# The fold of the output weights in three fp32r products instead of f32, its rows split ahead of it, the pooled rows loaded before the transforms, and frequency row 64 stored over GpSimd's queue

## The chip, the cores and the metric

One core of one Trainium2 chip runs the whole program. The metric is the device time of one execution in microseconds; a kernel's number is the median of its runs.

## The reference

The block works on two sequences, 2048 and 1024 tokens of width 1024, with the same weights:

```
h = rmsnorm(x, g1);  z = h @ w_in
za = z[:, :512] in 4 heads of 128:   f = real(fft2(za over tokens and channels));  ya = f @ w_fourier[h]
zb = z[:, 512:] in 4 groups of 128:  yb = ((mean over a window) - zb) @ w_pool[g] * pool_scale
x = x + concat(ya, yb) @ w_out
h = rmsnorm(x, g2);  x = x + (silu(h @ w_gate) * (h @ w_up)) @ w_down
y = rmsnorm(x, gf)
```

## The kernel before

All 3072 tokens pass through five stages in one program, and each engine has one instruction stream through all of them: input projection (`project_in`), Fourier mixing (`mix`), output projection (`project_out`), and the FFN (`ffn`). Nearly all products are made in three fp32r parts: a factor is rounded to fp32r by ScalarE (`hi`), VectorE subtracts that from the raw value (`lo`), and `three_products` adds hi·hi, hi·lo and lo·hi on TensorE, one instruction each.

The change lies in `mix`. It runs over eight units n = 0 to 7: four of the long sequence, four of the short one. A unit is a block of 128 rows (half the frequencies, cosine or sine part, of two heads) over all tokens of its sequence. VectorE folds its tokens (`fold`), TensorE transposes the folds (`turn_folds`), ScalarE and VectorE split them (`round_uv`, `rest_of_uv` write `uv_hi`, `uv_lo`), and TensorE multiplies them by tables at levels 0, 1, the base and, for the long sequence, 2 (`level_products`, `transform`). ScalarE copies the results to the unit's slot (`zy`, `zy_late`), and SyncE stores the slot to `y_scr` in HBM (`store_unit`). The slots of units 4 to 7 are loaded on SyncE's queue once the pooled values (`win`, stored over GpSimd's queue) have landed.

Between the parts of the units TensorE makes side products, in the order of `SIDE`, placed by `EARLY_SIDE` and `LATE_SIDE`, both indexed by unit:

- `F00` to `F31` and `G00` to `G31` fold the Fourier weights and the pooling weights into the rows of `w_out`: 16 products of 128x128 by 128x512, Fij for head i and column half j, Gij for pooling group i. Their left factors are `spread_w` and `wp_t`, their right ones the rows `wm` (mixed) and `wb` (pooled) of `w_out`. They are made in f32, two TensorE instructions each, on line 1324. ScalarE copies the F products (line 1196), VectorE the G products (line 1241). They go to two banks in turn, so a product waits for the copy of the one two before it (F01 for that of F00). The copies of F go to memory that the slots of units 0 and 1 hold, so they wait for these units' stores (`y_stored[0]`).
- `lone0` and `lone1` are the Fourier transform of frequency row 64 of the channels, which is stored apart from the units: TensorE, then GpSimd's four small multiplications, TensorE, TensorE; `store_lone` puts it into `y_scr` with four small DMAs on SyncE's queue, just before the stores of unit 3 and of unit 7.

The folded rows are split as well (`round_w` on ScalarE, `rest_of_w` on VectorE, lines 1202 and 1234; in `project_out` lines 1599 and 1809), and so is the first tile of y (`y_hi`, `y_lo`, lines 1218 and 1246), which is loaded from `y_scr` (line 1142) once units 0 to 3 and row 64 of the long sequence are stored. `project_out` begins on TensorE when `y_lo` and the first of the eight row blocks of weights are split, and takes them one by one. Each engine does its part in the order written in `scalar`, `vector`, `tensor`, `sync` and `gpsimd`.

Of the kernel before, what the change touches and what calls it, by code (L numbers as in the profile page):

```python
# [23 lines left out]
F32 = mybir.dt.float32  # L24
# [4 lines left out]
P = 128  # L29
# [827 lines left out]
class Mixer:  # L857
# [7 lines left out]
    FIRST_OF_TWO = 7  # L865
    EARLY_SIDE = ((), (1,), (3,), (4,), (6, 7), (11, 12), (16, 17), (20, 21))
# [3 lines left out]
    def __init__(self, nc, ahead, ctx, w_out, w_fourier, channel, z_scr, pool_gain, g2):  # L870
# [41 lines left out]
        self.wm = sb("wm", [P, HEADS, D], F32, ahead.w_place + 32 * K)  # L912
        self.chan = sb("chan", [P, channel_places().join1.stop - P], F32, ahead.folds_at)
# [10 lines left out]
        self.wm_loaded = sem("wm_loaded")  # L924
        self.wb_loaded = sem("wb_loaded")
# [60 lines left out]
    def load_mixed_rows(self, sp):  # L986
        sp.dma_start(self.wm[:, :, :], self.sources[0][0:HEADS * P, :].rearrange("(h p) n -> p h n", p=P)).then_inc(self.wm_loaded, DMA)

    def load_pooled_rows(self, sp):
        sp.dma_start(self.wb[:, :, :], self.sources[0][HEADS * P:, :].rearrange("(g p) n -> p g n", p=P)).then_inc(self.wb_loaded, DMA)  # L990
# [64 lines left out]
def mix(nc, ctx, ahead, mixer, z_scr, y_scr, w_pool):  # L1055
# [16 lines left out]
    spread_w = sb("spread_w", [P, HEADS, P], F32, 59 * K + 512)  # L1072
    MS = [S // P for S in SEQS]
# [11 lines left out]
    wm_loaded, wb_loaded = mixer.wm_loaded, mixer.wb_loaded  # L1085
    pool_w_loaded = sem("pool_w_loaded")
    lone_chain = sem("lone_chain")
    lone_turned = sem("lone_turned")
# [10 lines left out]
    def sync(sp):  # L1099
        def store_lone(q):  # L1100
            S, m = SEQS[q], MS[q]
            mixer.wait_side(sp, SIDE.index(f"lone{q} c"))
            for h in range(HEADS):
                sp.dma_start(y_scr[h, HALF_P, tok0[q]:tok0[q] + S].rearrange("(a b) -> a b", a=m),  # L1104
                             lone_out[q][h * m:(h + 1) * m, :]).then_inc(lone_stored[q], DMA)

        def store_unit(n):
            q, u = divmod(n, UNITS)
            S, k = SEQS[q], u % 2
            sp.wait_ge(out_done, mixer.stage(n, 3 - q))  # L1110
            for side in range(2):
                sp.dma_start(y_scr[u // 2 * 2 + side, k * (HALF_P + 1):(k + 1) * HALF_P, tok0[q]:tok0[q] + S],  # L1112
                             mixer.slot(n)[side * HALF_P + k:(side + 1) * HALF_P, :]).then_inc(y_stored[n // 2], DMA)

        sp.wait_ge(ahead.z_ready, TOKENS // HALF * KT)
        sp.dma_start(wp[:, :, :], w_pool.rearrange("g c d -> c g d")).then_inc(pool_w_loaded, DMA)
        for s in range(HEADS):
            sp.wait_ge(ahead.z_stored[s], TOKENS // HALF * DMA)
        for i in range(2):
            sp.wait_ge(ahead.d_stored[i], 2 * (TOKENS // HALF) * DMA)  # L1120
        sp.wait_ge(ahead.group_done, 4 * (TOKENS // HALF))
        mixer.load_unit(sp, z_scr, 1, 0)
        mixer.load_unit(sp, z_scr, 1, 1)
        for n in range(N):
            if n == UNITS - 1:
                store_lone(0)
            if n == N - 1:
                store_lone(1)
            store_unit(n)
            if n == 0:  # L1130
                mixer.load_unit(sp, z_scr, 1, 2)
                mixer.load_unit(sp, z_scr, 1, 3)
                mixer.load_lone(sp, 1)
            if n == 1:
                mixer.load_pooled_rows(sp)
            if n == UNITS - 1:
                for pair in range(2):
                    sp.wait_ge(y_stored[pair], 4 * DMA)
                sp.wait_ge(lone_stored[0], HEADS * DMA)
                for t in range(4):  # L1140
                    src = y_scr[:, :, t * P:(t + 1) * P].rearrange("c p s -> p c s")
                    sp.dma_start(y_raw[t // 2][:, :, t % 2 * P:(t % 2 + 1) * P], src).then_inc(ahead.y_loaded, DMA)

    def gpsimd(pool):
        done = 0
        for q in range(2):
# [6 lines left out]
            done += 2  # L1153
            pool.wait_ge(lone_chain, done)
            pool.tensor_tensor(g[:, 0:m], a[:, 0:m], a[:, m:], ALU.subtract).then_inc(lone_turned, 1)
            pool.tensor_tensor(g[:, m:], b[:, 0:m], b[:, m:], ALU.add).then_inc(lone_turned, 1)
            pool.wait_ge(lone_turned, 2 * q + 2)

    def scalar(act):
# [43 lines left out]

        for n in range(N):
# [11 lines left out]
            if n == N - 1:  # L1216
                act.wait_ge(ahead.y_loaded, 4 * DMA)
# [10 lines left out]
        round_w(1)  # L1228
        round_w(2)

    def vector(dve):
# [16 lines left out]

        for n in range(N):
# [6 lines left out]
            if n == N - 1:  # L1256
                rest_of_w(0)
                rest_of_y()
# [7 lines left out]
        rest_of_w(1)  # L1266

    def tensor(pe):
# [15 lines left out]
        def side(a):  # L1284
# [18 lines left out]
            elif name[0] == "l":  # L1303
# [6 lines left out]
                elif name[-1] == "b":  # L1310
                    pe.wait_ge(lone_turned, 2 * q + 2)
# [5 lines left out]
            else:  # L1317
                i, c = int(name[1]), int(name[2])
                if name == "F00":
                    pe.wait_ge(wm_loaded, DMA)  # L1320
                if name == "G00":
                    pe.wait_ge(wb_loaded, DMA)
                left, right = (spread_w, wm) if name[0] == "F" else (wp_t, wb)
                mm = pe.matmul(ps[:, :], left[:, i, :], right[:, i, c * HALF:(c + 1) * HALF], start=True, stop=True)
# [1734 lines left out]
```

## Time and profile before

| | us |
|---|---|
| median of 3 runs | 2498.29 (2497.23 to 2500.4) |
| the profiled execution | 2496.63 |
| its span | 2494.8 |
| TensorE busy | 2477.2 |
| VectorE busy | 1670.7 |
| ScalarE busy | 957.8 |
| GpSimd busy | 162.3 |

The span is the part of the execution that the profile covers; 1.8 us lie around it. The granted clock of TensorE was 0.999 of full speed over the span. All times below are from the span's start; the units' transforms lie from 291 us to 342 us. A matmul's duration covers its way through the array, so neighbours overlap: the cost of one is the step from its start to the next one's. ScalarE's and VectorE's instructions overlap a little too.

### The profile page before, as it was taken

Reading aid. Unit: us, or ns where it says so; the run is one execution under the profiler, and the core shown is the slowest. Engines: PE = TensorE matmul, PEld = TensorE weight load, DVE = VectorE, ACT = ScalarE, POOL = GpSimd, SP = SyncE. Lnnn points to the kernel's source line nnn. Section 1 sums busy time; section 2 is a strip of 40 time slices with the busy share of each in tenths; the row PEclk is TensorE's granted clock in tenths of the full one; section 3 lists DMA queues with packets and bytes.
Section 4 is the critical chain, followed back from the end, with each engine's and each line's share of the span. In section 5 each row is a group of like instructions: output and inputs, shape, how many; then the busy total and the mean of one; then the engine's idle time right before and its main releaser. Section 6 shows DMA issues by size and latency. Waiting matters only on the chain.

```text
span 2494.8 us, 32121 instructions
## 1 busy us (share of the span) xinstructions
PE 2477.2 (99%) x11133; PEld 2047.8 (82%) x11133; DVE 1670.7 (67%) x2595; ACT 957.8 (38%) x1825; POOL 162.3 (7%) x214
## 2 busy tenths in 40 slices
PE   9999999999999999999999999999999999999998
PEld 7888878887888888888888888888888888888887
DVE  5555678778767677777677686776764564455565
ACT  5533466667333333433333343333332232233333
POOL 2655400000000000000000000000000000000000
PEclk9999999999999999999999999999999999999999
DMA  6433667667323233432232442222346654354554
GB/s 184 115 84 99 212 218 248 239 239 277 136 100 109 97 109 110 182 126 109 80 117 99 155 157 96 110 109 80 126 177 220 239 207 168 114 199 147 191 193 148
DMA packets 154309, 381.99 MB, mean 153 GB/s; under 512 B 11928, under 2 KB 48120, under 8 KB 145012
## 3 DMA queue, kind: packets, MB, share of 16 engines
q1 hardware_dynamic: 145808, 350.86, 40.6%
q0 software_dynamic: 7984, 29.89, 3.2%
q8 instruction: 51, 0.84, 0.1%
q14 instruction: 34, 0.28, 0.0%
q10 hardware_dynamic: 432, 0.14, 0.0%
HBM read 254.22 MB, written 126.62 MB: 153 GB/s over the span
## 4 chain that ended last, share of the span: by engine, by line
PE 95%; DVE 2%; DMA 1%; issue 1%; ACT 1%; SPq 1%; DVEq 0%
PE bank L351 31%; PE bank L352 31%; PE bank L353 31%; PE bank L1968 1%; DMA a_raw<-ha_scr 0%; DMA y_scr<-zy_late 0%; DVE a_lo L2540 0%; DMA y_raw<-y_scr 0%; PE bank L765 0%; DMA xin<-in_x 0%; SPq L1112 0%; SPq L1104 0%; DVE x L1769 0%; ACT a_hi L2349 0%; PE bank L1039 0%
## 5 line engine op out<-in xcount | busy, mean ns | idle before, releaser
L351 PE MATMUL bank<-a_hi,w_hi 128*128 128x512 f32 x1848 | 719.5, 389 | 2.4 <-DVE w_lo L2551 1.6
L353 PE MATMUL bank<-a_hi,w_lo 128*128 128x512 f32 x1848 | 719.0, 389 | 0.0
L352 PE MATMUL bank<-a_lo,w_hi 128*128 128x512 f32 x1848 | 718.9, 389 | 0.0
L351 PEld LDWEIGHTS bank<-a_hi,w_hi 128*128 128x128 f32 x1848 | 346.9, 188 | 76.4 <-DVE w_lo L2551 2.8
L353 PEld LDWEIGHTS bank<-a_hi,w_lo 128*128 128x128 f32 x1848 | 346.9, 188 | 72.3
L352 PEld LDWEIGHTS bank<-a_lo,w_hi 128*128 128x128 f32 x1848 | 346.9, 188 | 71.6
L351 PE MATMUL bank<-t_hi,s_hi 128*128 128x512 f32 x924 | 359.4, 389 | 0.0
L352 PE MATMUL bank<-t_lo,s_hi 128*128 128x512 f32 x924 | 359.4, 389 | 0.0
L353 PE MATMUL bank<-t_hi,s_lo 128*128 128x512 f32 x924 | 359.4, 389 | 0.0
L2362 ACT ACTIVATE w_hi<-t_raw 128x512 fp32r<-128x512 f32 x256 | 162.0, 633 | 463.0 <-PE bank L353 379.5
L2701 DVE TENSOR_TENSOR s_lo<-s_raw,s_hi 128x512 fp32r<-128x512 f32 x231 | 156.2, 687 | 232.7 <-ACT s_hi L2437 232.6
L2437 ACT ACTIVATE s_hi<-s_raw 128x512 fp32r<-128x512 f32 x231 | 133.4, 620 | 320.6 <-DMA s_raw<-s_scr 320.6
L353 PEld LDWEIGHTS bank<-t_hi,s_lo 128*128 128x128 f32 x924 | 173.5, 188 | 36.0
L352 PEld LDWEIGHTS bank<-t_lo,s_hi 128*128 128x128 f32 x924 | 173.5, 188 | 36.0
L351 PEld LDWEIGHTS bank<-t_hi,s_hi 128*128 128x128 f32 x924 | 173.5, 188 | 36.0
L2551 DVE TENSOR_TENSOR w_lo<-t_raw,w_hi 128x512 fp32r<-128x512 f32 x256 | 176.0, 688 | 30.0 <-ACT w_hi L2362 26.3
L2551 DVE TENSOR_TENSOR w_lo<-w_raw,w_hi 128x512 fp32r<-128x512 f32 x192 | 132.1, 688 | 87.6 <-ACT w_hi L2362 87.5
L2362 ACT ACTIVATE w_hi<-w_raw 128x512 fp32r<-128x512 f32 x192 | 120.2, 626 | 121.3 <-PE bank L353 121.0
L351 PE MATMUL bank<-h_hi,win_hi 128*128 128x512 f32 x380 | 149.5, 394 | 0.0
L353 PE MATMUL bank<-h_hi,win_lo 128*128 128x512 f32 x380 | 148.0, 389 | 0.0
L352 PE MATMUL bank<-h_lo,win_hi 128*128 128x512 f32 x380 | 147.9, 389 | 0.0
L2322 POOL DMA_DIRECT2D acc<-x_scr x6 | 4.5, 754 | 1655.2 <-PE bank L353 1655.2
(266 smaller groups left out, 3143.3 us busy)
## 6 DMA issues: line engine op xcount, KB each, us to landing
s_scr<-sums_out SPq DMA_DIRECT2D x33, 1792.0 KB, 5.9
s_raw<-s_scr SPq DMA_DIRECT2D x42, 1024.0 KB, 5.1
w_raw<-in_w_gate SPq DMA_DIRECT2D x64, 512.0 KB, 3.6
w_raw<-in_w_up SPq DMA_DIRECT2D x64, 512.0 KB, 4.4
wd_staged<-in_w_down SPq DMA_DIRECT2D x121, 256.0 KB
a_raw<-ha_scr SPq DMA_DIRECT2D x21, 1024.0 KB, 4.9
s_raw<-s_scr SPq DMA_DIRECT2D x21, 768.0 KB, 4.7
x<-in_x SPq DMA_DIRECT2D x24, 512.0 KB, 4.5
```

Of the source, the lines that this page charges most:

```text
L351: pe.matmul(out, w_hi, m_hi, start=first, stop=False, **checks)
L352: pe.matmul(out, w_hi, m_lo, start=False, stop=False, **checks)
L353: return pe.matmul(out, w_lo, m_hi, start=False, stop=last, **checks)
L1968: mm = pe.transpose(t_ps[(slot % 2) * 2 + k][:, i, :], xn[:, slot % 2, d * P:(d + 1) * P], eye[:, :])
L2322: pool.dma_start(acc[b][half][:, :, :], src).then_inc(acc_loaded[b][half], DMA)
L2362: act.activation(w_hi[j][:, :], src, ACT.Copy).then_inc(w_hi_done, 1)
L2437: act.activation(s_hi[c][:, k - 4 * c, :], s_raw[c][:, k - 4 * c, :], ACT.Copy).then_inc(s_hi_done, 1)
L2551: dve.tensor_tensor(w_lo[j][:, :], src, w_hi[j][:, :].bitcast(F32), ALU.subtract).then_inc(w_ready, 1)
L2701: dve.tensor_tensor(s_lo[c][:, k - 4 * c, :], s_raw[c][:, k - 4 * c, :], s_hi[c][:, k - 4 * c, :].bitcast(F32), ALU.subtract).then_inc(s_r ...
```

## The change

- The left factors and the rows are split before use: ten pieces (`ROWS_SPLIT`), `spread` and `wp` of 512 columns, four blocks of mixed and four of pooled rows, 1024 columns each. ScalarE rounds (`round_rows`), VectorE subtracts (`rest_of_rows`), both at the end of the unit that `SPLIT_AT` names. `lo` parts are written over the raw values.
- Each of the 16 side products is made by `three_products`, three instructions.
- The pooled rows (`wb`, 2 MB) are issued on SyncE's queue behind `wp`, before the queue waits for the pooled values and loads units 4 to 7; before they were issued after the store of unit 1. Mixed and pooled rows share a semaphore, and the second load waits for the first.
- The four small stores of row 64 of each sequence are issued by GpSimd, after its multiplications, when the last copy of `lone` is made.
- `round_w(1)` moves ahead of the rounding of y in unit 7, `rest_of_w(0)` from unit 7 to the end of unit 6, `rest_of_w(1)` from behind unit 7's copies to ahead of the split of y.

```diff
+    ROWS_SPLIT = ("spread", "mixed0", "mixed1", "mixed2", "wp", "mixed3", "pooled0", "pooled1", "pooled2", "pooled3")
+    SPLIT_AT = ((0, 1), (2,), (3, 4), (5,), (6,), (7, 8), (9,), ())
...
     def load_pooled_rows(self, sp):
+        sp.wait_ge(self.rows_loaded, DMA)
...
         sp.dma_start(wp[:, :, :], w_pool.rearrange("g c d -> c g d")).then_inc(pool_w_loaded, DMA)
+        mixer.load_pooled_rows(sp)
         for s in range(HEADS):
             sp.wait_ge(ahead.z_stored[s], TOKENS // HALF * DMA)
...
-            if n == UNITS - 1:
-                store_lone(0)
-            if n == N - 1:
-                store_lone(1)
             store_unit(n)
...
-            if n == 1:
-                mixer.load_pooled_rows(sp)
...
     def gpsimd(pool):
+                pool.dma_start(y_scr[h, HALF_P, tok0[q]:tok0[q] + S].rearrange("(a b) -> a b", a=m),
+                               lone_out[q][h * m:(h + 1) * m, :]).then_inc(lone_stored[q], DMA)
...
             if n == N - 1:
+                round_w(1)
                 act.wait_ge(ahead.y_loaded, 4 * DMA)
...
+            for r in mixer.SPLIT_AT[n]:
+                round_rows(r)
-        round_w(1)
         round_w(2)
...
+        def rest_of_rows(r):
+            raw, hi, lo = rows_split(r)
+            dve.wait_ge(rows_hi_done, r + 1)
+            dve.tensor_tensor(lo, raw, hi.bitcast(F32), ALU.subtract).then_inc(rows_ready, 1)
...
             if n == N - 1:
-                rest_of_w(0)
+                rest_of_w(1)
                 rest_of_y()
...
-        rest_of_w(1)
+            for r in mixer.SPLIT_AT[n]:
+                rest_of_rows(r)
+            if n == N - 2:
+                rest_of_w(0)
...
-                mm = pe.matmul(ps[:, :], left[:, i, :], right[:, i, c * HALF:(c + 1) * HALF], start=True, stop=True)
+                rows = mixer.ROWS_SPLIT.index(("mixed" if name[0] == "F" else "pooled") + name[1])
+                pe.wait_ge(rows_ready, rows + 1)
+                    mm = three_products(pe, ps[:, :], spread_hi[:, i, :], spread_lo[:, i, :], mixer.wm_hi[:, i, of],
+                                        mixer.wm_lo[:, i, of], True, True)
```

VectorE, from the splits of unit 6's second group to the first weights of `project_out`, before (`uv_lo` is the split of folds, `wout_raw_94` a copy of a G product, `wout_lo` a split of folded rows):

```order
L1051 TENSOR_TENSOR uv_lo_120<-bank,uv_hi_118 128x384 [waits uv_hi_done]
L1241 TENSOR_SCALAR wout_raw_94<-bank 128x512 [waits side_made] x2
L1051 TENSOR_TENSOR uv_lo_121<-bank,uv_hi_119 128x256 [waits uv_hi_done]
L1241 TENSOR_SCALAR wout_raw_94<-bank 128x512 [waits side_made]
L1051 TENSOR_TENSOR uv_lo_121<-bank,uv_hi_119 128x384 [waits uv_hi_done]
L1241 TENSOR_SCALAR wout_raw_94<-bank 128x512 [waits side_made] x3
L1234 TENSOR_TENSOR wout_lo_107<-wout_raw_93,wout_hi 128x2x512 [waits wout_hi_done]
L1246 TENSOR_TENSOR y_lo_113<-y_raw_51,y_hi_109 128x1024 [waits y_hi_done]
L1241 TENSOR_SCALAR wout_raw_94<-bank 128x512 [waits side_made] x2
L1234 TENSOR_TENSOR wout_lo_107<-wout_raw_93,wout_hi 128x2x512 [waits wout_hi_done]
```

and now (line 1283 is the split of the rows, 1272 the copy, 1265 and 1277 the splits of folded rows and of y):

```order
L1057 TENSOR_TENSOR uv_lo_120<-bank,uv_hi_118 128x384 [waits uv_hi_done]
L1272 TENSOR_SCALAR wout_raw_94<-bank 128x512 [waits side_made] x2
L1283 TENSOR_TENSOR wb_lo<-wb,wb_hi 128x1024 [waits rows_hi_done] x2
L1057 TENSOR_TENSOR uv_lo_121<-bank,uv_hi_119 128x256 [waits uv_hi_done]
L1272 TENSOR_SCALAR wout_raw_94<-bank 128x512 [waits side_made]
L1057 TENSOR_TENSOR uv_lo_121<-bank,uv_hi_119 128x384 [waits uv_hi_done]
L1272 TENSOR_SCALAR wout_raw_94<-bank 128x512 [waits side_made] x2
L1283 TENSOR_TENSOR wb_lo<-wb,wb_hi 128x1024 [waits rows_hi_done]
L1265 TENSOR_TENSOR wout_lo_107<-wout_raw_93,wout_hi 128x2x512 [waits wout_hi_done]
L1272 TENSOR_SCALAR wout_raw_94<-bank 128x512 [waits side_made]
L1265 TENSOR_TENSOR wout_lo_107<-wout_raw_93,wout_hi 128x2x512 [waits wout_hi_done]
L1277 TENSOR_TENSOR y_lo_113<-y_raw_51,y_hi_109 128x1024 [waits y_hi_done]
```

Three splits of pooled rows stand between the G copies, and both first splits of folded rows stand ahead of the split of y.

SyncE's queue, from `wp` to the load of y, before (`zy_95` is the slot of units 4 to 7, `lone_out` row 64):

```order
L1116 DMA wp<-in_w_pool 128x4x128 [waits z_ready]
L967 DMA zy_95<-z_scr 64x1024 [waits d_stored0,z_stored3,d_stored1,z_stored2,group_done,z_stored1,z_stored0]
L1112 DMA y_scr<-zy 64x2048 [waits out_done]
L967 DMA zy_95<-z_scr 64x1024 x4
L1112 DMA y_scr<-zy 63x2048 [waits out_done]
L990 DMA wb<-in_w_out 128x4x1024
L1112 DMA y_scr<-zy_late 64x2048 [waits out_done]
L1104 DMA y_scr<-lone_out_129 16x128 [waits side_done]
L1104 DMA y_scr<-lone_out_129 16x128 x3
L1112 DMA y_scr<-zy_late 63x2048 [waits out_done]
L1142 DMA y_raw_51<-y_scr 128x8x128 [waits lone_stored0,y_stored1,y_stored0]
```

and now:

```order
L1132 DMA wp<-in_w_pool 128x4x128 [waits z_ready]
L996 DMA wb<-in_w_out 128x4x1024 [waits rows_loaded]
L972 DMA zy_95<-z_scr 64x1024 [waits d_stored0,z_stored3,d_stored1,z_stored2,group_done,z_stored1,z_stored0]
L1128 DMA y_scr<-zy 64x2048 [waits out_done]
L972 DMA zy_95<-z_scr 64x1024 x4
L1128 DMA y_scr<-zy 63x2048 [waits out_done]
L1128 DMA y_scr<-zy_late 64x2048 [waits out_done]
L1128 DMA y_scr<-zy_late 63x2048 [waits out_done]
L1153 DMA y_raw_51<-y_scr 128x8x128 [waits lone_stored0,y_stored1,y_stored0]
```

The load of the pooled rows has gone from between the stores of units 1 and 2 to ahead of the loads of units 4 to 7, and the stores of row 64 have left the queue. (A second DMA of the same kind behind a row, without a wait of its own, is left out here.)

## Rows read from the trace of the kernel before

**Rows 1.** The page's busy time by engine: us (share of the span) x instructions

```profile
PE 2477.2 (99%) x11133; PEld 2047.8 (82%) x11133; DVE 1670.7 (67%) x2595; ACT 957.8 (38%) x1825; POOL 162.3 (7%) x214
```

**Rows 2.** Waits from 190 to 360 us: engine, line, releaser, total us, times, longest

```profile
PE bank L1324 <- ACT wout_raw L1196: 2.0, 1, 2.0
...
PE bank L351 <- DVE wout_lo L1234: 0.7, 1, 0.7
PE bank L351 <- DVE y_lo L1246: 0.6, 1, 0.6
...
PE bank L1324 <- DVE wout_raw L1241: 0.2, 1, 0.2
```

**Rows 3.** ScalarE in order of time, in brackets its idle time and who ended it

```profile
312.63 0.64 ACT L1172 ACTIVATE zy_late<-bank 128x512 f32<-128x512 f32 x1 [1.30 <-PE bank L353]
...
318.59 0.60 ACT L1196 ACTIVATE wout_raw<-bank 128x512 f32<-128x512 f32 x1 [2.10 <-DMA y_scr<-zy]
...
333.66 1.04 ACT L1202 ACTIVATE wout_hi<-wout_raw 128x1024 fp32r<-128x1024 f32 x1
...
339.93 1.06 ACT L1218 ACTIVATE y_hi<-y_raw 128x1024 fp32r<-128x1024 f32 x1 [1.84 <-DMA y_raw<-y_scr]
```

**Rows 4.** The issue of DMAs on SyncE's queue in order of time

```profile
299.88 2.37 SPq L967 DMA_DIRECT2D zy<-z_scr  x4
...
309.71 0.79 SPq L1112 DMA_DIRECT2D y_scr<-zy  x2
310.54 0.77 SPq L990 DMA_DIRECT2D wb<-in_w_out  x1
...
315.97 4.24 SPq L1104 DMA_DIRECT2D y_scr<-lone_out  x4
...
331.20 3.66 SPq L1142 DMA_DIRECT2D y_raw<-y_scr  x4
```

**Rows 5.** Line 1324 over the span: count, duration ns min/median/max, first and last start

```profile
L1324 PE MATMUL bank<-wm,spread_w x16: 592/592/697, 315.3 to 329.1; 128*128 128x512 f32 x16
```

**Rows 6.** TensorE in order of time: start, us, engine, line, operation, tiles, count

```profile
309.62 0.47 PE L351 MATMUL bank<-tab_hi,uv_hi 128*128 128x512 f32 x1
309.93 0.39 PE L352 MATMUL bank<-tab_lo,uv_hi 128*128 128x512 f32 x1
...
311.97 0.39 PE L352 MATMUL bank<-tab_lo,uv_hi 128*128 128x512 f32 x1
...
322.43 2.83 PE L1324 MATMUL bank<-wm,spread_w 128*128 128x512 f32 x6
...
325.23 0.28 PE L352 MATMUL bank<-tab_lo,uv_hi 128*128 128x256 f32 x1
325.34 0.28 PE L353 MATMUL bank<-tab_hi,uv_lo 128*128 128x256 f32 x1
...
336.50 0.28 PE L352 MATMUL bank<-tab_lo,uv_hi 128*128 128x256 f32 x1
...
342.30 0.50 PE L351 MATMUL bank<-wout_hi,y_hi 128*128 128x512 f32 x1 [0.57 <-DVE y_lo L1246]
```

**Rows 7.** DMA issues, 283 to 284 us

```profile
y_scr<-win POOLq DMA_DIRECT2D x1, 260.0 KB, 5.6
```

**Rows 8.** DMA issues, 296 to 297 us

```profile
y_scr<-win POOLq DMA_DIRECT2D x1, 260.0 KB, 2.9
```

**Rows 9.** VectorE in order of time

```profile
305.48 0.68 DVE L1013 TENSOR_TENSOR scratch<-zy 128x512 f32<-128x512 f32 x1
...
308.61 0.69 DVE L1051 TENSOR_TENSOR uv_lo<-bank,uv_hi 128x512 fp32r<-128x512 f32 x1 [0.26 <-ACT uv_hi L1045]
...
344.49 5.76 DVE L1809 TENSOR_TENSOR wout_lo<-wout_raw,wout_hi 128x1024 fp32r<-128x1024 f32 x5
```

**Rows 10.** 2 us stretches: PE, PEld, DVE, ACT, POOL busy, TensorE's clock, DMA share, GB/s

```profile
294.00:296.00 2.00, 2.00 (x20) 2.00 (x18) 0.51 (x1) 2.00 (x5) 1.84 (x3) 1.00 0.18 55
```

**Rows 11.** DMA issues, 310.5 to 311 us: count, KB, us to landing

```profile
wb<-in_w_out SPq DMA_DIRECT2D x1, 2048.0 KB, 13.4
```

More of the change, by code:

```diff
@@ L1072, in mix @@
     spread_w = sb("spread_w", [P, HEADS, P], F32, 59 * K + 512)
+    wp_lo = sb("wp_lo", [P, 4, P], F32R, 61 * K + 512)
+    wp_hi = sb("wp_hi", [P, 4, P], F32R, 29 * K + 512)
+    spread_lo = sb("spread_lo", [P, HEADS, P], F32R, 59 * K + 512)
+    spread_hi = sb("spread_hi", [P, HEADS, P], F32R, 52 * K + 512)
     MS = [S // P for S in SEQS]
@@ L1099, in sync @@
     def sync(sp):
[L1100 to L1105, printed above, removed]
         def store_unit(n):
@@ L1144, in gpsimd, with store_lone @@
     def gpsimd(pool):
-        done = 0
+        def store_lone(q):
+            S, m = SEQS[q], MS[q]
+            mixer.wait_side(pool, SIDE.index(f"lone{q} c"))
+            for h in range(HEADS):
+                pool.dma_start(y_scr[h, HALF_P, tok0[q]:tok0[q] + S].rearrange("(a b) -> a b", a=m),
+                               lone_out[q][h * m:(h + 1) * m, :]).then_inc(lone_stored[q], DMA)
         for q in range(2):
@@ L1152, in gpsimd @@
             pool.tensor_tensor(b, cs, turn[:, m:3 * m], ALU.mult).then_inc(lone_chain, 1)
[L1153 to L1157, printed above, removed]
+            pool.wait_ge(lone_chain, 4 * q + 2)
+            pool.tensor_tensor(g[:, 0:m], a[:, 0:m], a[:, m:], ALU.subtract).then_inc(lone_chain, 1)
+            pool.tensor_tensor(g[:, m:], b[:, 0:m], b[:, m:], ALU.add).then_inc(lone_chain, 1)
+            pool.wait_ge(lone_chain, 4 * q + 4)
+            store_lone(q)
     def scalar(act):
@@ L1202, in round_w, with round_rows @@
             act.activation(w_hi[:, :, d, :], w_raw[0][:, :, d, :], ACT.Copy).then_inc(ahead.w_hi_done, 1)
+        def round_rows(r):
+            name = mixer.ROWS_SPLIT[r]
+            raw, hi, _ = rows_split(r)
+            if name == "mixed0":
+                act.wait_ge(rows_loaded, DMA)
+            elif name == "pooled0":
+                act.wait_ge(rows_loaded, 2 * DMA)
+            elif name in ("spread", "wp"):
+                mixer.wait_side(act, SIDE.index(name))
+            act.activation(hi, raw, ACT.Copy).then_inc(rows_hi_done, 1)
         for n in range(N):
@@ L1318, in side @@
                 i, c = int(name[1]), int(name[2])
[L1319 to L1323, printed above, removed]
-                mm = pe.matmul(ps[:, :], left[:, i, :], right[:, i, c * HALF:(c + 1) * HALF], start=True, stop=True)
+                rows = mixer.ROWS_SPLIT.index(("mixed" if name[0] == "F" else "pooled") + name[1])
+                pe.wait_ge(rows_ready, rows + 1)
+                of = slice(c * HALF, (c + 1) * HALF)
+                if name[0] == "F":
+                    mm = three_products(pe, ps[:, :], spread_hi[:, i, :], spread_lo[:, i, :], mixer.wm_hi[:, i, of],
+                                        mixer.wm_lo[:, i, of], True, True)
+                else:
+                    mm = three_products(pe, ps[:, :], wp_hi[:, i, :], wp_lo[:, i, :], mixer.wb_hi[:, i, of],
+                                        mixer.wb_lo[:, i, of], True, True)
             mm.then_inc(side_made, 1)
```

28 lines of the change are left out of this document (21 added, 7 removed).

## The prediction

> **What bounds the kernel now.** The page's busy times come first: TensorE is at work in 2477.2 of 2494.8 us [rows 1]. So the kernel can gain in two ways: less work on TensorE, or fewer stalls of it. The waits of the stretch from 190 to 360 us show the stalls: 2.0 us on ScalarE's copies of folded rows, 0.7 on the split of folded rows, 0.6 on the split of y and 0.2 on a copy of VectorE [rows 2], 3.5 us in all. Everything the change touches lies there. After that the timelines of the engines say what stands behind each stall.
>
> The largest is F01's. It waits for the copy of F00, and ScalarE began that only at 318.59, after 2.10 us of waiting for the store of unit 1 to land [rows 3]. That store was issued at 309.71, with the 2 MB of pooled rows right behind it [rows 4]. The wait on y has the same origin: y's load began at 331.20 [rows 4] and ScalarE took it at 339.93, again after waiting for a DMA [rows 3].
>
> **The products.** There are 16 of them; the mixed half stands in the trace as 16 matmuls of 592 ns, two for each product [rows 5], the pooled half likewise. Their cost is the step, not the duration. Six such instructions (three products) begin at 322.43, the second instruction of the next group begins at 325.23, and a 256-column step is 0.11 to 0.12 us [rows 6]. So three products take 2.80 - 0.12 = 2.68 us, one takes 0.89. In fp32r a 512-column step is (311.97 - 309.93) / 9 = 0.227 us [rows 6], three are 0.68. That saves 0.21 us a product, 16 x 0.21 = 3.4 us on TensorE's own path. The wait for the split rows adds to that only where a split is late, which is counted below.
>
> **The stalls that go.** Without the pooled rows, the store of unit 1 and that of unit 2 share the queues with nothing new. From 309.71 to 331.20 the queue moved three stores of about 1 MB and the 2 MB of rows: 5 MB in 21.5 us. Three fifths of that is 12.9 us, so units 1 to 3 are stored by about 323 instead of 331. Unit 1's store, landed at 318.6 before, should land near 315.5; F00's product ends at about 316.3, so F01's 2.0 us go. If none of this came true and unit 1 landed at 318.5 again, 1.9 us of stall would stay: that is the other end of this term. The 4.24 us in which the queue issued row 64's four stores [rows 4] go as well. y's load then begins at 323 and lands, with the 8.7 us of before (331.20 to 339.93), at about 332. ScalarE asks for it at 336. It is hidden with 4 us to spare, and even a load that lands at 338 costs only 0.1. The waits on y, on the first folded rows and on the copy (0.6 + 0.7 + 0.2) go in their old form. Gone: 3.5 us.
>
> GpSimd issues row 64's stores from about 314.3, in some 2.3 us of its own. Pooled values over this queue landed 2.9 to 5.6 us after issue [rows 7, 8], so row 64 is there by 322.5, just ahead of unit 3's store; 5 us more would still be hidden. The store of row 64 of the short sequence is as free: before, it stood in front of the store of unit 7.
>
> **The pooled rows in their new place.** Now 2 MB are in flight from 292.5, when the last pooled values are still to be stored, and the queue may load units 4 and 5 only when these have landed: issued at 296.8, landed 2.9 us later [rows 8]; the queue went on at 299.88 [rows 4]. The DMA engines have room, 18% busy from 294 to 296 [rows 10], so I let the rows be in by 299.5 and keep unit 4's arrival at about 305: cost 0. At a busy time the same kind of store took 5.6 us [rows 7]; the cost of that is rival 1.
>
> The Trainium skill speaks against this move. Its page "DMA: Bandwidth & Descriptors", section "SWDGE vs HWDGE vs iDMA", has each DMA engine take its hardware-fed and software-fed queues in turn, so the small store would share with the rows in front of it rather than pass or queue behind them. By that rule it is about 1 us late while the rows last, unit 4 comes at 306, and the sum below would be -2.0 instead of -3.0.
>
> **The stalls that come.** The ten splits cost ScalarE 0.95 to 1.04 us for each of the eight blocks of 1024 columns [rows 3] and VectorE 5.76 / 5 = 1.15 us [rows 9]. They are put at the ends of units, where ScalarE waits for TensorE anyway: 1.30 us before 312.63 [rows 3] cover most of unit 2's 1.5. VectorE is tighter, and I followed the three engines from unit to unit with these durations (the same reckoning, done for the kernel before, ends within 0.3 us of the trace).
>
> - Unit 1's split lies between the fold of unit 4 and the split of unit 3's folds at 308.61, before which VectorE idled 0.26 us [rows 9]. It comes 0.9 us later; TensorE, which took it at 309.62 [rows 6], had 0.3 us in hand. With 0.1 won before that: 0.4 us of stall.
> - G10 needs pooled block 1, whose subtraction stands behind the copy of G01. After G01, TensorE has 1.07 us of other work; VectorE needs 0.2 to see the product, 0.6 for the copy (a 512-column instruction is 0.69 long [rows 9]) and 1.15: 0.9 us of stall.
> - From the end of G20 to the first product of `project_out` TensorE has little work and VectorE much. Before, 336.38 (the row at 336.50 less one step) to 342.30 [rows 6] held 5.9 us, of which 0.8 idle; less 3 x 0.21 for three products, 4.5 us of work remain. VectorE must in this time split unit 7's folds, copy G11 and G20 (0.6 each), split block 3 (1.15), split w0 (1.15), copy G21 (0.6), split w1 (1.15) and then y (1.2): with the small waits for ScalarE, 6.7 us. So 2.2 us of stall, most of it on `y_lo`. Behind it nothing more is late: w2 is split before its turn at 2.7 us after the start, so the 0.7 of before has no heir.
> - Small ones at F21, G01 and around the copies: 0.4 us.
>
> Sum of the new ones: 0.4 + 0.9 + 2.2 + 0.4 = 3.9 us.
>
> **The sum.** -3.4 (products) - 3.5 (old stalls) + 3.9 (new stalls) = -3.0 us. The profiled execution of 2496.6 would become 2493.6. It lies 1.7 us under the median of the runs shown, so for the median I take 2498.3 - 3.0 = 2495.3. Later stages are TensorE's without a gap of this kind, so the 3.0 us should stay.
>
> **The rivals.** All of them turn on the new place of the pooled rows or on VectorE.
>
> 1. The pooled rows hold up the pooled values. With 5.6 us for that last store [rows 7] unit 4 comes 2.7 us late. VectorE began its fold at 305.48 [rows 9] and would begin at 307; that delays unit 3's split and TensorE by 2.0 us. Result -1.0: 2497.3.
>
> 2. The other side: the pooled rows take the 13.4 us that they took before [rows 11] and are in flight to 306. Loads of units 4 and 5 share with them and unit 4 lands at 309. Each us past 305 costs one us on TensorE, since fold, split and level 0 of unit 3 stand in one line; break-even is at 308. At 309 the result is +1.0, and with the stores behind them late too (unit 1 at 321) +1.5: 2499.8.
>
> 3. More is won than I reckon, since the new stalls on VectorE are my own reckoning and no row shows them. If only half of the 3.9 us came, the result would be -5.0: 2493.3. Against it: the order on VectorE leaves no room between G20 and y.
>
> 4. The change doesn't do what it says: the three-part product takes as long as the f32 one, 0.89. Then nothing is saved, but the stalls shrink too, since TensorE comes later to each of them: -0.9, 2497.4. Against it stand 9 steps in a row of 0.227 with new weights for each [rows 6].
>
> **How the numbers follow.** Forecast 0.50, rival 1 0.19, rival 2 0.13, rival 3 0.15, rival 4 0.03. What a measurement of this kernel can tell from no change is about 0.2%, 5.0 us; the runs before lie 3.2 us apart. Only rival 3 at its far end reaches that downwards: 0.11. Upwards only rival 2 with everything late: 0.04. Same: 0.85. The range goes down to rival 3 and a little below, for the scatter, 2492.3, and up to rival 2, 2499.9.
>
> **What would show it.** In the changed kernel's trace: line 1324's f32 products gone, three steps of 0.227 in their place; no wait of ScalarE for a DMA before the copy of F00, nor before `y_hi`; a stall near 0.9 us before G10 and one of 1 to 2 us on `y_lo` before `project_out`; the first product of `project_out` at about 340.1 (before 342.30), without the gap of 0.7 us after it. I am wrong if VectorE waits for unit 4's load, if GpSimd's stores of row 64 hold up y, or if the stall on `y_lo` is missing or above 3 us.

## The result, and the profile after

The changed kernel takes 2501.68 us (median of 22 runs, 2498.45 to 2505.49), the kernel before in the same batch 2497.76 (22 runs, 2496.31 to 2501.4): ratio 1.0015, 95% interval 1.0009 to 1.0021. It is slower by about 3.9 us; 2495.3 was forecast, with 2499.9 as the upper end. The profiled execution took 2500.15 us, its span 2498.4, 3.6 more than before.

TensorE's busy time has hardly changed against [rows 1], by the page:

```profile
PE 2476.6 (99%) x11149; PEld 2051.5 (82%) x11149; DVE 1682.0 (67%) x2605; ACT 965.7 (39%) x1835; POOL 165.4 (7%) x222
```

So the time has gone into stalls. TensorE's waits from 290 to 350 us (line, releaser, total us, times, longest) answer to [rows 2]:

```profile
PE bank L1045 <- DVE uv_lo L1057: 2.9, 1, 2.9
PE bank L351 <- ACT wout_raw L1213: 1.6, 1, 1.6
PE bank L351 <- DVE y_lo L1277: 1.3, 1, 1.3
PE bank L351 <- DVE wb_lo L1283: 1.1, 1, 1.1
PE bank L351 <- DVE wout_raw L1272: 0.3, 2, 0.2
PE bank L1354 <- DVE wout_raw L1272: 0.3, 1, 0.3
PE bank L351 <- DVE uv_lo L1057: 0.2, 1, 0.2
```

They come to 7.7 us, against 3.5. The largest is one that the forecast had at 0.4. F01's wait (the second row) should have gone and is still 1.6. F01 waits for the copy of F00, the product right before it: up to F10 the side products share one bank, and only from then on do they wait for the copy of the one two before.

What stands behind the first is seen on SyncE's queue, in order of time, beside [rows 4]:

```profile
292.51 0.57 SPq L996 DMA_DIRECT2D wb<-in_w_out  x1
302.97 2.38 SPq L972 DMA_DIRECT2D zy<-z_scr  x4
...
312.91 0.79 SPq L1128 DMA_DIRECT2D y_scr<-zy  x2
...
330.94 3.65 SPq L1153 DMA_DIRECT2D y_raw<-y_scr  x4
```

The loads of units 4 and 5 are issued 3.1 us later than before (299.88), and the store of unit 1 3.2 us later. y's load begins where it did. The DMA issues from 285 to 330 us (KB each, us from issue to landing) say why; they answer to [rows 8, 11]:

```profile
wb<-in_w_out SPq DMA_DIRECT2D x1, 2048.0 KB, 10.7
...
y_scr<-win POOLq DMA_DIRECT2D x1, 260.0 KB, 6.3
...
y_scr<-lone_out POOLq DMA_DIRECT2D x4, 8.0 KB, 3.8
```

The pooled rows need 10.7 us, to 303.2. The last store of the pooled values, issued at 296.48, falls into their time and takes 6.3 us instead of 2.9, and SyncE may not load unit 4 before it has landed. It landed at 302.8, about when the rows did. So VectorE, which had no wait there in [rows 9], waits for unit 4:

```profile
307.73 0.69 DVE L1019 TENSOR_TENSOR scratch<-zy 128x512 f32<-128x512 f32 x1 [2.07 <-DMA zy<-z_scr]
```

TensorE in order of time, beside [rows 6]:

```profile
312.49 0.41 PE L1045 MATMUL bank<-eye,zy_late 128*128 128x128 f32 x2 [2.95 <-DVE uv_lo L1057]
312.65 0.48 PE L351 MATMUL bank<-tab_hi,uv_hi 128*128 128x512 f32 x1
...
313.43 0.47 PE L351 MATMUL bank<-tab_hi,uv_hi 128*128 128x512 f32 x1
313.70 0.63 PE L352 MATMUL bank<-tab_lo,uv_hi 128*128 128x512 f32 x1
...
316.69 0.56 PE L353 MATMUL bank<-tab_hi,uv_lo 128*128 128x512 f32 x1
317.08 0.38 PE L1045 MATMUL bank<-eye,zy 128*128 128x128 f32 x2
...
347.13 0.50 PE L351 MATMUL bank<-wout_hi,y_hi 128*128 128x512 f32 x1 [1.30 <-DVE y_lo L1277]
```

After the stall of 2.95 us the steps grow from 0.23 to 0.43 us. The nine matmuls from 313.43 to 317.08 take 3.65 us, where nine steps of 0.227 would take 2.04: 1.6 us more. The windows of this kernel (busy us by engine, granted clock, DMA share, GB/s) name the reason in the column PEclk: the clock granted in 314 to 316 us is 0.50, so 1.2 GHz instead of 2.4.

```profile
312.00:314.00 2.00, 1.51 (x7) 1.33 (x8) 1.46 (x4) 1.07 (x2) 0.00 (x0) 0.91 1.03 248
314.00:316.00 2.00, 2.00 (x6) 1.54 (x6) 1.90 (x5) 0.78 (x2) 0.00 (x0) 0.50 1.11 239
316.00:318.00 2.00, 2.00 (x10) 1.31 (x9) 2.00 (x4) 0.72 (x2) 0.00 (x0) 0.74 0.93 286
322.00:328.00 6.00, 4.62 (x25) 3.75 (x26) 4.60 (x10) 5.39 (x13) 0.00 (x0) 1.00 0.56 199
```

Hold on to the last row: while TensorE and the queue wait for stores, the DMA engines are at 0.56.

Which of these delays sets the time? The stall and the slow steps make TensorE 4.5 us late, but behind them it still waits 1.56 us at F01, for a copy that waits for unit 1's store. ScalarE's copy of F00 and TensorE's F01, first before (F00's copy is in [rows 3]), then in the changed kernel:

```profile
319.24 1.98 PE L1324 MATMUL bank<-wm,spread_w 128*128 128x512 f32 x4 [2.01 <-ACT wout_raw L1196]
```

```profile
322.61 0.60 ACT L1213 ACTIVATE wout_raw<-bank 128x512 f32<-128x512 f32 x1 [1.45 <-DMA y_scr<-zy]
323.26 0.50 PE L351 MATMUL bank<-wm_hi,spread_hi 128*128 128x512 f32 x1 [1.56 <-ACT wout_raw L1213]
```

The copy and F01 are both 4.02 us later than before. So there are two late paths from the same cause. One goes over unit 4, VectorE and the stall; alone it would have brought F01 at 321.7. The other goes over SyncE's queue, whose store of unit 1 was issued 3.2 us late and took 9.7 us instead of 8.9; it brought F01 at 323.26. The second is the longer by 1.56 us, so it sets the time from F01 on.

### The profile page after: what moved, and what is told of

The parts are those of the page before. It is cut to its first block, busy times and chain, and to the rows that moved or that the text cites. A ratio compares the mean times of both kernels' runs of the same rounds, so it can differ in the third digit from the quotient of the medians.

```text
span 2498.4 us, 32187 instructions
## 1 busy us (share of the span) xinstructions
PE 2476.6 (99%) x11149; PEld 2051.5 (82%) x11149; DVE 1682.0 (67%) x2605; ACT 965.7 (39%) x1835; POOL 165.4 (7%) x222
## 4 chain that ended last, share of the span: by engine, by line
PE 93%; DMA 2%; DVE 2%; ACT 1%; POOL 1%; issue 1%; SPq 0%; POOLq 0%; ACTq 0%; DVEq 0%
PE bank L351 30%; PE bank L353 30%; PE bank L352 30%; DMA y_scr<-win 1%; PE bank L2010 1%; DVE a_lo L2582 0%; DMA tab_raw<-in_table 0%; POOL win L322 0%; DMA y_scr<-zy 0%; ACT a_hi L2391 0%; SPq L972 0%; PE bank L765 0%; DMA xin<-in_x 0%; DMA a_raw<-ha_scr 0%; POOL win L332 0%
```

## The experiments

Each is against the kernel before, run in the same batch on the same chip; experiments 1 to 4, 5 to 8, 9 to 11 and 12 are four batches, so that runs of different batches are compared by their ratios. "After" is the changed kernel.

**1. Rows at the old place.** After, with the pooled rows loaded behind unit 1's store again:

```diff
-        mixer.load_pooled_rows(sp)
...
+            if n == 1:
+                mixer.load_pooled_rows(sp)
```

> The changed kernel with the pooled rows issued after the store of unit 1, as before; all else of the change stays. Theory 1 (the rows, in flight from 292.5 us, hold up the last pooled values, so the queue, unit 4's load, its fold and TensorE are late, and the long idle time halves TensorE's clock): no VectorE wait for unit 4's load, the 2.95 us stall and the stretch at clock 0.5 gone, median 1 us under the kernel before, about 5 us under the changed one. Theory 2 (the new splits on VectorE cause the long stall, since unit 1's split stands between the fold and unit 3's split): the stall stays near 3 us and the time within 1 us of the changed kernel's. Theory 3 (GpSimd's stores of row 64 hold up the rest): the same, time as the changed kernel's.

Measured 2498.95 us, ratio 1.0003 (0.9994 to 1.0012). The rows' early place costs 2.7 us of the 3.9; the two intervals overlap a little, and experiment 2 has the same cause clear of noise. Theory 1 is right about the stall and the clock, but not in size: 1 us under the kernel before was expected, and it is 1.3 above, within noise. TensorE's wait for `uv_lo` is 0.7 and its clock 1.00 throughout.

**2. Rows early, nothing else.** Before, with only this move:

```diff
+        sp.wait_ge(mixer.wm_loaded, DMA)
+        mixer.load_pooled_rows(sp)
...
-            if n == 1:
-                mixer.load_pooled_rows(sp)
```

> The kernel before with one thing changed: the pooled rows issued behind wp. Theory 1: the last store of pooled values lands about 6 us after issue instead of 2.9, the queue goes on at 303, VectorE waits 2 us for unit 4, TensorE about 2 us; if that idle time also halves the clock, 1.7 us more: 2 to 4 us over the kernel before. Theory 2: no loss, since no split is added; the time of before or 1 us less, as the rows are out of the way of the units' stores.

Measured 2502.86, ratio 1.0018 (1.0009 to 1.0027): the move alone costs about 5 us, where Theory 1 had 2 to 4. The path over unit 4 is shorter than expected: the last store of pooled values takes 5.1 us, VectorE waits 1.1, TensorE 0.8 with its clock at 1.00. The price is paid on the other path. This is ScalarE's wait before it copies F00:

```profile
ACT wout_raw L1196 <- DMA y_scr<-zy: 5.4, 1, 5.4
```

Unit 1's store was issued at 311.65 and landed at 322.5, although nothing but other stores stood behind it. TensorE waited 5.3 us for F00's copy.

**3. The products alone.** Experiment 1, with row 64 stored over SyncE's queue as before; no part of the change but the products and their splits is left:

```diff
-            store_lone(q)
...
+            if n == UNITS - 1:
+                store_lone(0)
+            if n == N - 1:
+                store_lone(1)
```

> The three-part products and their splits alone: pooled rows in their old place and row 64 on SyncE's queue. Theory 1: close to the run with the rows in their old place, 0 to 1 us under the kernel before: products -3.4 us, new stalls on VectorE about +3.9, of the old stalls the one on F01 stays near 1.7. Theory 3: clearly faster than the run that has row 64 on GpSimd's queue, by 1 us or more.

Measured 2497.75, ratio 0.9998 (0.9989 to 1.0007): zero. Against experiment 1 (2498.95) GpSimd's queue for row 64 isn't shown to gain or to cost anything. TensorE's largest waits here:

```profile
PE bank L351 <- ACT wout_raw L1217: 2.2, 1, 2.2
PE bank L351 <- DVE y_lo L1281: 1.3, 1, 1.3
PE bank L351 <- DVE wb_lo L1287: 1.1, 1, 1.1
PE bank L1045 <- DVE uv_lo L1057: 0.7, 1, 0.7
```

All its waits sum to 6.0 us, 2.5 more than before, and the span is 0.3 longer. So the products save about 2.2 in this execution.

**4. TensorE kept busy.** After, with 13 idle matmuls where TensorE waits for unit 3's split:

```diff
+                if n == 2 and g == 2:
+                    pe.wait_ge(out_done, mixer.stage(1, 0))
+                    for _ in range(13):
+                        pe.matmul(bank[1][:, :], tab_hi[:, 0:P], tab_hi[:, 0:HALF], start=True, stop=True)
```

> The changed kernel with 13 additional matmuls of 128x128 by 128x512 that nothing uses, 13 x 0.227 = 2.95 us, on TensorE where it waits for unit 3's split. Theory 1 with the clock as a part of the loss: the clock stays at 1.00 from 313 to 317 us, level 0 of unit 3 steps 0.227 us all through instead of 0.43, time about 1.7 us under the changed kernel. If the slow steps have another cause (transfers, reads of the tables), they stay at 0.43 and the time is that of the changed kernel.

Measured 2502.39, ratio 1.0017 (1.0008 to 1.0026). The clock is 1.00 from 308 to 320 us and no step is 0.43, but nothing is won. The test is a weak one: in this execution VectorE waited only 1.3 us for unit 4 (2.07 in after), so the stall that the idle matmuls filled would have been shorter. And what they can win ends at F01, which waits for unit 1's store whatever TensorE did before:

```profile
PE bank L351 <- ACT wout_raw L1213: 2.8, 1, 2.8
```

The wait is 2.78 us here and 1.56 in after. The half clock is real in after's profiled execution, but by the trace it cost nothing there: without its 1.6 us TensorE would have waited 1.6 us longer at F01.

**5. No pooled rows at all.** Before, without their load; the pooled products take columns of the table instead:

```diff
-            if n == 1:
-                mixer.load_pooled_rows(sp)
...
-                if name == "G00":
-                    pe.wait_ge(wb_loaded, DMA)
-                left, right = (spread_w, wm) if name[0] == "F" else (wp_t, wb)
-                mm = pe.matmul(ps[:, :], left[:, i, :], right[:, i, c * HALF:(c + 1) * HALF], start=True, stop=True)
+                left, right = (spread_w, wm) if name[0] == "F" else (wp_t, None)
+                idle = mixer.places[mixer.plan_of(N - 1)["levels"][0], "sin"]
+                rows = right[:, i, c * HALF:(c + 1) * HALF] if right is wm else tab_hi[:, idle:idle + HALF].bitcast(F32)
+                mm = pe.matmul(ps[:, :], left[:, i, :], rows, start=True, stop=True)
```

> The kernel before without the load of the pooled rows (2 MB); the products of the pooled groups take 512 columns of the table as their right factor instead, of the same size and kind, so the last four row tiles of the output weight are wrong and nothing else changes in work. Theory A, that of the prediction: the rows behind unit 1's store slow it and all that follows, so without them it lands near 315.5 us, F01's wait (2.0 us before) goes and the load of y starts at 323 instead of 331: 2494.5 us, 3.3 us less. Theory B, from the runs so far: what is issued behind a store doesn't slow it, and the stores of units 1 and 3 are slow by themselves (63 rows each, DMA share near 0.58 for 8 us): unit 1's store lands at 318 and later as before, F01's wait stays within 0.5 us, the load of y starts at 328 or later; within 1 us of before.

Measured 2499.84, ratio 1.0006 (0.9997 to 1.0015). Theory A falls: ScalarE waits for unit 1's store longer than before, and y's load begins at 328.47 instead of 331.20, not at 323.

```profile
ACT wout_raw L1194 <- DMA y_scr<-zy: 3.9, 1, 3.9
```

Theory B is right that the rows aren't what slows the store, and wrong in size: issued at 309.52, it landed at 320.4, 1.8 us later than with the rows behind it. Where unit 2's store follows directly (here, in experiments 2 and 4 and in after) it took 9.7 to 10.9 us from issue, with the rows between (before, experiments 1 and 3) 8.9 to 9.6. Why is open. The kernel's median is not shown to differ from before's.

**6. Stores of 48 and 15 rows.** Before, with each 63-row store of the odd units cut in two, and the waits on the stores raised from 4 to 6 to match:

```diff
-                sp.dma_start(y_scr[u // 2 * 2 + side, k * (HALF_P + 1):(k + 1) * HALF_P, tok0[q]:tok0[q] + S],
-                             mixer.slot(n)[side * HALF_P + k:(side + 1) * HALF_P, :]).then_inc(y_stored[n // 2], DMA)
+                for a, b in (((1, 49), (49, HALF_P)) if k else ((0, HALF_P),)):
+                    sp.dma_start(y_scr[u // 2 * 2 + side, k * HALF_P + a:k * HALF_P + b, tok0[q]:tok0[q] + S],
+                                 mixer.slot(n)[side * HALF_P + a:side * HALF_P + b, :]).then_inc(y_stored[n // 2], DMA)
```

> The kernel before with each 63-row store of the odd units issued as 48 and 15 rows. 
Measured 2494.81, ratio 0.9989 (0.9980 to 0.9998): 2.6 us faster, with an interval from 0.5 to 5.0. The window from 322 to 326 us, first of before, then of this kernel, shows DMA share and GB/s at the end:

```profile
322.00:326.00 4.00, 4.00 (x20) 2.39 (x19) 2.61 (x6) 3.04 (x7) 0.00 (x0) 1.00 0.59 239
```

```profile
322.00:326.00 4.00, 4.00 (x22) 2.81 (x22) 3.04 (x7) 3.12 (x9) 0.00 (x0) 1.00 1.03 408
```

The share rises from 0.59 to 1.03 and the rate from 239 to 408 GB/s: this is what one expects if the stores of 63 rows used nine of sixteen engines (9/16 is 0.56). ScalarE takes F00 at 316.67 instead of 318.59, TensorE's wait for it is 0.4, and y's load starts at 328.84. The waits of 0.6 and 0.7 us around `y_lo` were expected to go; 0.3 and 0.7 are left. The Trainium skill has the rule, in "DMA: Bandwidth & Descriptors", section "Why a DMA increments its semaphore by 16 and not by 1": a hardware-fed DMA takes the largest number of engines, up to 16, that divides the slowest dimension of both its sides. For 63 that is 9, for 48 it is 16, for 15 it is 15. With its shares of 0.59 and 1.03 the trace agrees, but it doesn't show 48 and 15 apart, and no run cuts the 63 rows otherwise: that the row counts help, and not just that there are two transfers for one, rests on this rule and on the 0.59.

**7. Rows behind unit 5.** After, with the pooled rows issued after the loads of units 4 and 5:

```diff
         mixer.load_unit(sp, z_scr, 1, 1)
+        mixer.load_pooled_rows(sp)
```

> The kernel after with the pooled rows issued behind the loads of units 4 and 5 (near 300 us) instead of ahead of them. If they cost by holding up the last store of the pooled values and with it unit 4 (6.3 us against 2.9 to landing, unit 4 at 308 against 305.5): the store lands in 3 us again, VectorE doesn't wait for unit 4, TensorE's 2.95 us wait for uv_lo and its half clock go, 3 us off: 2498.5 us. Rival: 2 MB more ahead of unit 0's and unit 1's stores hold these up, F01's wait of 1.6 us grows to 4 or more: no gain, 2501 us or more.

Measured 2503.82, ratio 1.0026 (1.0017 to 1.0035). The rival was right. The pooled values' store lands in 2.3 us and VectorE doesn't wait for unit 4, but 2 MB now stand ahead of the stores of units 0 and 1, and unit 1's lands 16.1 us after its issue:

```profile
PE bank L351 <- ACT wout_raw L1213: 6.0, 1, 6.0
```

With one path mended and the other made longer, the kernel is slower: the store's path is the one that counts here. The rows ahead of a store delayed it in each of these runs; these two moves only chose who pays.

**8. Products and 48 and 15 rows.** Experiment 3 with the edit of 6, its core being

```diff
+                for a, b in (((1, 49), (49, HALF_P)) if k else ((0, HALF_P),)):
```

> Three-part products alone (pooled rows at their old place, row 64 over SyncE's queue: 0.0 us against before) with the stores of 48 and 15 rows. If the 63-row stores hold up y and F01: the waits for wout_raw (2.2 us) and y_lo (1.3 us) go while the products' 3.4 us stay, wb_lo's 1.1 us remains: 2493.5 us, 4 less than before. If they don't: 2497.7 as without the split.

Measured 2496.42, ratio 0.9996 (0.9987 to 1.0005), where 2493.5 was expected. It is 1.6 us more than the stores alone, with overlapping intervals. F01's wait is gone, those for `y_lo` (1.3) and `wb_lo` (1.1) are unchanged: `y_lo` is late by VectorE's own order here, not by the load of y.

**9. Splits at other places.** Experiment 8 with

```diff
-    SPLIT_AT = ((0, 1), (2,), (3, 4), (5,), (6,), (7, 8), (9,), ())
+    SPLIT_AT = ((0, 1, 2), (3,), (4, 5), (), (6, 7), (8, 9), (), ())
```

> As the run with three-part products and stores of 48 and 15 rows, but with the ten splits behind other units: pieces 0 to 2 behind unit 0, 3 behind unit 1, 4 and 5 behind unit 2, 6 and 7 behind unit 4, 8 and 9 behind unit 5. There TensorE still waited 1.3 us for y_lo, 1.1 for wb_lo of the second pooled block, 0.7 for uv_lo and 0.7 in small pieces. If the place of the splits is what costs: the 1.1 for wb_lo goes, about 1 us off: 2495.4 us against 2496.4. If it is the work itself on VectorE and ScalarE, which has no free place: the waits turn up elsewhere (uv_lo of units 3 and 5, y_lo) with the same sum, 2496.4 us.

Measured 2494.88, ratio 0.9987 (0.9978 to 0.9996). The interval overlaps that of 8, so a gain from the places isn't shown. The waits moved: `wb_lo` is gone, `y_lo` 0.6, while 0.9 for a copy of VectorE and 0.7 for copies of ScalarE came.

**10. Only the mixed rows in three parts.** Experiment 8 with the pooled products in f32 again, and the splits of the mixed rows at the places of experiment 9:

```diff
-    SPLIT_AT = ((0, 1), (2,), (3, 4), (5,), (6,), (7, 8), (9,), ())
+    SPLIT_AT = ((0, 1, 2), (3,), (4,), (), (), (), (), ())
...
-                    mm = three_products(pe, ps[:, :], wp_hi[:, i, :], wp_lo[:, i, :], mixer.wb_hi[:, i, of],
-                                        mixer.wb_lo[:, i, of], True, True)
+                    pe.wait_ge(rows_loaded, 2 * DMA)
+                    mm = pe.matmul(ps[:, :], wp_t[:, i, :], wb[:, i, of], start=True, stop=True)
```

> Stores of 48 and 15 rows, and three-part products for the mixed rows (F) alone: the eight pooled products (G) stay f32 and the splits of wp and of the pooled rows go (4.9 us of VectorE less). If the splits' work is what ate the gain: 1.6 us for the F products stay (8 x 0.2), the waits for wb_lo (1.1) and most of that for y_lo (1.3 to 0.3) go: 2493.5 us, 1.3 less than the stores alone (2494.8). Rival: the two halves are alike and the F half's splits cost what they save too (uv_lo 0.7 and small ones): 2494.8, as the stores alone.

Measured 2493.50, ratio 0.9984 (0.9975 to 0.9993). It has the lowest median of all, some 4 us under before, and hits the 2493.5 expected, though `y_lo` keeps 0.8 where 0.3 was expected. Its interval overlaps those of 8 and 9 and that of 6, with which it shared no batch, so that leaving out the pooled half gains isn't shown. Its waits from 290 to 350 us sum to 2.0:

```profile
PE bank L1045 <- DVE uv_lo L1057: 1.0, 1, 1.0
PE bank L351 <- DVE y_lo L1282: 0.8, 1, 0.8
PE bank L1370 <- DVE wout_raw L1277: 0.2, 1, 0.2
```

**11. After with 48 and 15 rows.** The same edit in the changed kernel, with the waits on the stores raised to match:

```diff
-                    sp.wait_ge(y_stored[pair], 4 * DMA)
+                    sp.wait_ge(y_stored[pair], 6 * DMA)
```

> The kernel after with the 63-row stores issued as 48 and 15 rows. If the early place of the pooled rows costs by delaying unit 4 and the stores alike: F01's wait (1.6 us) goes, while the wait for uv_lo of unit 3 (2.9 us) and the half clock behind it stay: 2499.5 us, 2 less than after and 2 more than before. Rival: with the stores quick the early rows cost nothing more: 2496.4 us, as the same kernel with the rows at their old place.

Measured 2498.91, ratio 1.0004 (0.9995 to 1.0013). As expected, F01's wait goes, and the 3.2 us for `uv_lo` stay, with a granted clock of 0.51 in 312 to 314 us. With the store's path shortened, the path over unit 4 is the one that counts.

**12. Half the rows early.** Experiment 11, with pooled row tiles 0 and 1 early and 2 and 3 behind unit 1's store (the second argument picks the half; the wait for the second load is left out here):

```diff
-        mixer.load_pooled_rows(sp)
+        mixer.load_pooled_rows(sp, 0)
...
+            if n == 1:
+                mixer.load_pooled_rows(sp, 1)
```

> The kernel after with stores of 48 and 15 rows (2498.9 us), but with only the first two pooled row tiles (1 MB) loaded early and the other two behind unit 1's store. If what costs is that 2 MB are still on their way when the last store of the pooled values is issued (296.5 us): 1 MB in some 5 us from 292.6 is in by then, the store lands in 3 us as before (6.3 with 2 MB), VectorE doesn't wait for unit 4 (2.4 us), the waits for uv_lo fall from 3.2 to 0.7: 2496.4 us, as with all rows at the old place. Rival: any rows at that place hold the store up, in proportion or wholly: 2497.5 to 2499 us.

Measured 2496.03, ratio 0.9992 (0.9983 to 1.0001), 2.9 us less than experiment 11, though in another batch and with intervals that just overlap. This is the DMA issue row of the last store of the pooled values:

```profile
y_scr<-win POOLq DMA_DIRECT2D x1, 260.0 KB, 2.7
```

VectorE doesn't wait for unit 4 and `uv_lo` costs 0.8. TensorE reaches F01 at 317.93, in experiment 11 at 321.59: 2.4 of these 3.7 us are the longer stall and 1.3 the slow steps behind it, since here no later wait hides them.

The expectation had the first MB in before the store is issued. It wasn't: it landed at 298.4 and the store was issued at 296.43. What the traces show is when the store lands. In all five kernels with an early load it lands within 0.7 us of the load's end: 302.8 and 303.2 in after, 301.8 and 301.5 in experiment 2, 301.8 and 301.7 in 4, 303.2 and 302.9 in 11, 299.1 and 298.4 in 12. So the early place is not wrong by itself; with 1 MB the load is over 2 us after the store's issue, which is within the 2.3 to 2.9 us that the store takes without it, and with 2 MB it lasts 5 to 7 us.

## Why the prediction was wrong

**The step that failed: "the rows be in by 299.5 and keep unit 4's arrival at about 305: cost 0".** They were in at 303.2 and the fold of unit 4 began at 307.73, which is the first sign of being wrong that the prediction names. The share of 18% from 294 to 296 us [rows 10] was not room for 2 MB in the 7 us from 292.5: in 294 to 296 us after moves 192 GB/s at a share of 0.86, and the store of the pooled values landed only when the rows did. The cause is that of rival 1, which put 5.6 us on that store [rows 7]; it took 6.3. The size is beyond rival 2, 3.9 us over before against its 1.5; its 13.4 us for the rows were 10.7. What the late store cost went two ways. Rival 1 priced the way over unit 4: 2.0 us on top of 0.4, measured 2.9 in the stall plus 1.6 in slow steps, which neither rival counted. But in after the other way sets the time, over the queue and unit 1's store, which landed at 322.6, 4.0 us later than before. Rival 2 named it, with unit 1 at 321. Experiments 2 and 7 show the second way, where TensorE waits 5.3 and 6.0 us at F01 and 0.8 and 0.7 on `uv_lo`; experiments 11 and 12 show the first. The rule of the Trainium skill that was weighed there ("DMA: Bandwidth & Descriptors", section "SWDGE vs HWDGE vs iDMA": hardware- and software-fed queues in turn) has the sign right, and the estimate of 1 us from it was too small against the 3.4 measured. The store landed as if it stood behind the rows and not as if it shared with them; why is open.

**"units 1 to 3 are stored by about 323 instead of 331", "so F01's 2.0 us go".** Wrong, and experiment 5 tests just this. The argument took the queue for a pipe that is shared by volume: 5 MB in 21.5 us, so 3 MB in 12.9. But the rows behind unit 1's store didn't slow it, and two of the three stores have 63 rows. [Rows 4] held the hint: 5 MB in 21.5 us are 233 GB/s, and a share of 0.59 beside stores in flight, which the windows of before show from 322 to 328 us, is no full pipe. Of the 3.5 us that should go, after kept F01's 1.6; the 0.7 behind the first product of `project_out` did go. So did ScalarE's wait for y, but not because y came early: its load began at 330.94, not at 323, and was hidden only because all else had become later.

**The products: -3.4 forecast.** The mechanism was right, the size was not. The step of 0.227 holds within a series, but the first step behind a transposition or a wait is 0.31 to 0.34. F00 and the 256-column step behind it took 0.98 us before and 0.88 in after:

```profile
315.27 1.02 PE L1324 MATMUL bank<-wm,spread_w 128*128 128x512 f32 x2
315.73 0.68 PE L351 MATMUL bank<-tab_hi,uv_hi 128*128 128x256 f32 x1
316.25 0.28 PE L352 MATMUL bank<-tab_lo,uv_hi 128*128 128x256 f32 x1
```

```profile
319.84 0.47 PE L351 MATMUL bank<-wm_hi,spread_hi 128*128 128x512 f32 x1
320.15 0.39 PE L352 MATMUL bank<-wm_lo,spread_hi 128*128 128x512 f32 x1
320.38 0.39 PE L353 MATMUL bank<-wm_hi,spread_lo 128*128 128x512 f32 x1
320.61 0.28 PE L351 MATMUL bank<-tab_hi,uv_hi 128*128 128x256 f32 x1
320.72 0.28 PE L352 MATMUL bank<-tab_lo,uv_hi 128*128 128x256 f32 x1
```

Eleven of the 16 products of after have such a first step and take 0.77 to 0.81 us, the others 0.70. Added up from the rows, the 16 take 12.1 us, and before 14.2. So 2.1 us are saved, close to the 2.2 of experiment 3. The 0.89 of the forecast holds as the mean of before; the 0.68 was taken from a row of long series, where the mean of after is 0.76.

**The new stalls: +3.9 forecast.** Right where they follow from VectorE's order: 0.9 before G10, measured 1.1; 2.2 between G20 and `y_lo`, measured 1.3 and 0.65 around copies, in a stretch of 6.9 us where 6.7 was reckoned (the durations listed there come to 6.45 even without the split of unit 7's folds); unit 3's split 0.4, measured 0.7 where unit 4 comes in time (experiments 1 and 3). Experiment 3, without a late unit 4, has them whole: 6.0 less F01's 2.2 is 3.8. So rival 3 (only half of them) falls, and rival 4 (the product as long as f32) with the products above.

**The sum, mended.** By what TensorE did up to 350 us: waits +4.2 (7.7 for 3.5), half clock +1.6, products -2.1: +3.7 us. The fifth product of `project_out` is 3.9 us late (349.99 for 346.12); the 0.2 between are short gaps that the list doesn't count. The span grew by 3.6. Against the forecast, 0.4 became 2.9 + 1.6, and -2.0 became -0.4; these two make up 5.7 of the 6.6 us between -3.0 and +3.6, the products another 1.3, and small ones give 0.4 back. This sum says where the time went, not what each cause would give back: the 1.6 of the half clock and the 2.9 of the stall lie ahead of F01's wait, and F01 began 4.0 us late by its store. From F01 on, products and new stalls cancel. **Row 64 over GpSimd** is as forecast in its effect: its stores were issued at 319.40 instead of 314.3 and landed 3.8 us after issue, in no one's way.

## What to carry to other kernels

Read the DMA share while the queue is the thing waited for: here a share near 9/16 with everybody waiting pointed to a transfer's shape that leaves engines idle, and cutting it (63 rows into 48 and 15) was the only single edit that made the kernel faster. Before a load is moved ahead, look for the small transfer that a later step waits on and ask how long the load lasts after that transfer is issued: 2 us were hidden here, 5 to 7 us were not. Follow a delay to the last wait that it meets. Filling a stall gains nothing where a later wait has another cause, as at F01. When matmuls are made cheaper with splits on other engines, count the waits that the splits bring: here they ate the whole gain of the products (experiment 3). That the mixed half, whose splits fall on freer engines, is better alone is suggested by experiment 10 and not shown.

## What was not expected of the hardware

- Long stalls of TensorE were followed by a stretch at half clock, shorter ones were not. Granted clock 0.50 after a stall of 2.95 us in after, 0.51 around 3.2 us in experiment 11, 0.50 in 322 to 324 us after 3.8 us in experiment 5, 0.51 in 324 to 326 us after 5.3 us in experiment 2, 0.50 in 324 to 328 us after 6.0 us in experiment 7. After 2.0, 2.2 and 2.8 us (before, experiments 3 and 4) it stayed at 1.00. The slow steps took 1.6 us more in after and 1.3 in experiment 11, and only in the latter was no wait behind them that hid it.
- A store of 260 KB over GpSimd's queue takes 2.3 to 2.9 us alone at this place and 5.1 to 6.4 us when it is issued 4 us behind a 2 MB load on the hardware queue; it lands within 0.4 us of that load.
- A 2 MB load issued right behind unit 1's store didn't make it land later: 8.9 to 9.6 us from issue with the load there, 9.7 to 10.9 with the next store in its place.
